# Differential attention: first row scaling, corner memset and scaling of the maximum left out, mask added on TensorE, squares on VectorE

## The reference

```python
q = partial_rope(rms_norm(q, q_norm_g), pos)
lam = exp(sum(lam_q1 * lam_k1)) - exp(sum(lam_q2 * lam_k2)) + lam_init
s = einsum('bqhd,bkhd->bhqk', q_blk, k) * DA_HEAD_DIM ** -0.5
allowed = k_chunk[None, :] <= q_chunk[:, None]        # chunks of 64 tokens
s = where(allowed, s, -inf)
p = softmax(s, axis=-1)                               # two maps per head pair
p = p[:, :, 0] - lam * p[:, :, 1]
o = einsum('bhqk,bkhe->bqhe', p, v)
o = rms_norm(o, subln_g, eps=1e-5) * (1.0 - lam_init)
return o.reshape(B, S, D) @ w_o
```

## Time and profile before

| what | value |
|---|---|
| median of 3 runs | 2335.53 us |
| lowest and highest | 2334.25 and 2338.73 us |
| the profiled execution, own time | 2339.69 us |
| its span in the trace | 2337.7 us |
| mean granted TensorE clock | 0.939 |
| PE, PEld busy | 2052.0, 1574.0 us |
| DVE, ACT, POOL busy | 795.4, 808.4, 857.0 us |

### The profile page before, as it was taken

One profiled execution on the slowest core, in us unless ns is written; L12 is line 12 of the kernel. 1 busy time (PEld: TensorE's weight loads), 2 busy tenths in 40 slices (PEclk: granted clock), 3 DMA queues, 4 the chain that ended last, 5 costly groups with the idle time before them and its releaser, 6 DMA issues.

```text
span 2337.7 us, 37067 instructions
## 1 busy us (share of the span) xinstructions
PE 2052.0 (88%) x15556; PEld 1574.0 (67%) x15556; DVE 795.4 (34%) x1209; ACT 808.4 (35%) x1051; POOL 857.0 (37%) x1112
## 2 busy tenths in 40 slices
PE   4897976668999999989997699999998999979897
PEld 3666866534777778865674377777887886748764
DVE  5487333334422221023447542222101133252333
ACT  6566232232334342132125434343212423242232
POOL 4263322210454545534330044545454523215430
PEclk8899999995999999999998789999999999889999
DMA  4101000020233333222110022333332211112110
GB/s 146 54 30 57 22 4 5 4 67 1 72 90 90 90 90 99 99 81 73 54 53 3 0 68 77 90 90 90 99 99 90 90 55 54 37 59 90 55 54 36
DMA packets 190707, 147.10 MB, mean 63 GB/s; under 512 B 6888, under 2 KB 188351, under 8 KB 190576
## 3 DMA queue, kind: packets, MB, share of 16 engines
q1 hardware_dynamic: 190576, 145.18, 20.3%
HBM read 143.06 MB, written 2.10 MB: 62 GB/s over the span
## 4 chain that ended last, share of the span: by engine, by line
PE 56%; issue 17%; POOL 14%; DVE 7%; ACT 5%; DMA 1%; SPq 0%; POOLq 0%; ACTq 0%; DVEq 0%
PE psum L2318 13%; POOL w_lo L1027 13%; PE psum L2320 12%; PE psum L2319 12%; PE psum L2481 4%; ACT w_hi L1159 1%; DVE X_lo L1692 1%; PE psum L2324 1%; PE psum L2743 1%; DVE col L2093 1%; PE psum L2706 1%; PE psum L2716 1%; PE psum L2394 1%; PE psum L2731 1%; PE psum L2900 1%
## 5 line engine op out<-in xcount | busy, mean ns | idle before, releaser
L1027 POOL TENSOR_TENSOR w_lo<-weight_raw,w_hi 128x256 fp32r<-128x256 f32 (+2 forms) x1048 | 772.0, 773 | 1227.7 <-ACT w_hi L1159 1227.5
L2318 PE MATMUL psum<-X_hi,w_hi 128*128 128x512 f32 x1528 | 633.2, 414 | 76.4 <-POOL w_lo L1027 42.1
L2320 PE MATMUL psum<-X_hi,w_lo 128*128 128x512 f32 x1528 | 608.4, 398 | 0.0
L2319 PE MATMUL psum<-X_lo,w_hi 128*128 128x512 f32 x1528 | 608.3, 398 | 0.0
L2318 PEld LDWEIGHTS psum<-X_hi,w_hi 128*128 128x128 f32 x1528 | 295.4, 193 | 184.0 <-issue 84.3
L1159 ACT ACTIVATE w_hi<-weight_raw 128x2048 fp32r<-128x2048 f32 (+2 forms) x134 | 249.6, 1863 | 376.5 <-PE psum L2320 364.0
L2319 PEld LDWEIGHTS psum<-X_lo,w_hi 128*128 128x128 f32 x1528 | 295.8, 194 | 64.8 <-issue 6.7
L2320 PEld LDWEIGHTS psum<-X_hi,w_lo 128*128 128x128 f32 x1528 | 294.6, 193 | 64.9
L1741 DVE TENSOR_TENSOR sgate<-rt,psum 128x512 f32<-128x512 f32 x44 | 30.2, 688 | 340.4 <-PE psum L2320 340.4
L2318 PE MATMUL psum<-hb_hi,w_hi 128*128 128x512 f32 x352 | 136.9, 389 | 0.0
L2319 PE MATMUL psum<-hb_lo,w_hi 128*128 128x512 f32 x352 | 136.9, 389 | 0.0
(11 more groups left out here) (447 smaller groups left out, 2624.3 us busy)
## 6 DMA issues: line engine op xcount, KB each, us to landing
weight_raw<-in_ffn_w_gu SPq DMA_DIRECT2D x88, 512.0 KB, 4.9
weight_raw<-in_l_w_in SPq DMA_DIRECT2D x45, 512.0 KB, 4.7
weight_raw<-in_ffn_w_down SPq DMA_DIRECT2D x40, 512.0 KB, 3.7
weight_raw<-in_kv_w SPq DMA_DIRECT2D x16, 512.0 KB, 4.0
weight_raw<-in_l_w_out SPq DMA_DIRECT2D x16, 512.0 KB, 4.0
weight_raw<-in_rw_w_k SPq DMA_DIRECT2D x8, 512.0 KB, 6.7
weight_raw<-in_rw_w_r SPq DMA_DIRECT2D x8, 512.0 KB, 4.0
weight_raw<-in_rw_w_v SPq DMA_DIRECT2D x8, 512.0 KB, 4.1
```

What stands on the lines that cost most here:

```text
L1027: ins = pool.tensor_tensor(l, r, h.bitcast(F32), ALU.subtract)
L2318: pe.matmul(ps, wh, xh, start=start, stop=False, skip_group_check=True)
L2319: pe.matmul(ps, wh, xl, start=False, stop=False, skip_group_check=True)
L2320: return pe.matmul(ps, wl, xh, start=False, stop=stop, skip_group_check=True)
```

## The change

The first row scaling goes: the first map stays as ACT's exponentials made it, and only the second is multiplied, by minus lambda times the first row sum over the second. The combined row is thereby larger by the first row sum. ACT writes that sum to a table `l1s`, and its square times 128e-5 enters the sum of squares as four small products on PE (`lsq`), in place of the constant epsilon. The memset of the corner goes: PE adds -1e30 there with a product of one row, the first row of the constant `blk` (64 ones, 64 zeros) by a row `neg` of 64 numbers, once for each map, behind both scores. The scaling of the maximum goes: the factor 1/8 moves into the gain of q's norm, and the reduction negates its own result. The squares of `oT` move from ACT to DVE, into the tiles of `aq`: seven of them into the loop, at the second query tile of a head pair from the third pair on, the last one behind it. PE adds up seven of the squares ahead of the last `values`, and the last one behind it.

```diff
--- before.py
+++ after.py
@@ -660,6 +660,9 @@
         PTs = a_("PTs", [P, 2, S])
         tq2 = a_("tq2", [P, 2, S])
         rth = a_("rth", [16, S])
+        l1s = a_("l1s", [P, TT, HEADS // 2])
+        lsq = a_("lsq", [P, TT, 16])
+        neg = a_("neg", [1, CH])
         n_hi = a_("n_hi", [16, S], F32R)
         n_lo = a_("n_lo", [16, S], F32R)
 
@@ -761,6 +764,7 @@
         rope_in, lam_in = sem("rope_in"), sem("lam_in")
         lam_row, lam_ready = sem("lam_row"), sem("lam_ready")
         sc_max = sem("sc_max")
+        lsq_ready = sem("lsq_ready")
         pc_ready = sem("pc_ready")
         hn_rot = sem("hn_rot")
 
@@ -1245,18 +1249,6 @@
                             last = act.activation(dst[:, 2 * i + m, 0:S], bank(b[m]), func)
                     last.then_inc(step_a, 1)
 
-            def head_scale(src, n, at, key, scale, eps, ready, count, hi):
-
-                for k in range(n):
-                    if k >= 2:
-                        act.wait_ge(hn_pe, hn_pe_count(at, k - 2))
-                    act.activation(xf[:, k % 2, :], src[:, k, 0:S], ACT.Square).then_inc(hn_a, 1)
-                wait_done(act, key)
-                act.activation(rt[0:16, :], psum[0:16, job_banks(key)[0], :], ACT.Sqrt, bias=cst[0:16, eps:eps + 1],
-                               scale=scale).then_inc(job_a, 1)
-                act.wait_ge(ready, count)
-                act.activation(hi[:, :], rt[0:16, :], ACT.Copy).then_inc(kn_h, 1)
-
             def layer_norm(n):
 
                 name = ("eo", "oo")[n]
@@ -1539,8 +1531,9 @@
                     for sub in range(2):
                         q = 2 * ((i + 2) % 3) + sub
                         ins = act.activation(Pb[:, q, 0:P * (tq + 1)], psum[:, b[sub], 0:P * (tq + 1)], ACT.Exp,
-                                             bias=col[:, 4 + q:5 + q], scale=HN ** -0.5,
-                                             accum_out=col[:, 16 + q:17 + q])
+                                             bias=col[:, 4 + q:5 + q],
+                                             accum_out=(l1s[:, tq, (i + 2) // TT:(i + 2) // TT + 1] if sub == 0 else
+                                                        col[:, 16 + q:17 + q]))
                     ins.then_inc(job_a, 1)
                 if i >= 0:
                     if i >= 1 and (i - 1) % TT == TT - 1:
@@ -1551,8 +1544,11 @@
                     act.activation(PTs[:, i % 2, 0:P * (tq + 1)], bank(job_banks(key)[0], P * (tq + 1)),
                                    ACT.Copy).then_inc(job_a, 1)
             empty(("ot", HEADS // 2 - 1), oT[:, HEADS // 2 - 1, :])
-            wait_job(act, ("ot", HEADS // 2 - 1))
-            head_scale(oT, KT, 16, ("osq",), 1.0 / P, C_EPS5, kn_f, 5, n_hi)
+            wait_done(act, ("osq",))
+            act.activation(rt[0:16, :], psum[0:16, job_banks(("osq",))[0], :], ACT.Sqrt, scale=1.0 / P
+                           ).then_inc(job_a, 1)
+            act.wait_ge(kn_f, 5)
+            act.activation(n_hi[:, :], rt[0:16, :], ACT.Copy).then_inc(kn_h, 1)
             for k in range(KT):
                 wait_job(act, ("oinv", k))
                 x_high1(XV["attn"], k, oT)
@@ -2020,6 +2016,8 @@
             wait_job(dve, ("lam",))
             link(dve.tensor_tensor(col[:, 2:3], col[:, 1:2], col[:, 0:1], ALU.subtract))
             dve.tensor_scalar(col[:, 3:4], col[:, 2:3], -LAM_INIT, None, ALU.add)
+            dve.memset(neg[0:1, :], -1e30)
+            dve.tensor_scalar(col[:, 13:14], pcol("da_q_norm_g"), HN ** -0.5, None, ALU.mult)
             link(dve.tensor_scalar(col[:, 12:13], pcol("da_subln_g"), 1.0 - LAM_INIT, None, ALU.mult))
 
             def scaled(name, dst, steps):
@@ -2049,7 +2047,7 @@
                                           ALU.subtract).then_inc(kn_l, 1)
                     elif what == "hinv":
                         wait_done(dve, key)
-                        dve.scalar_tensor_tensor(out=src[:, k, :], in0=src[:, k, :], scalar=pcol(g),
+                        dve.scalar_tensor_tensor(out=src[:, k, :], in0=src[:, k, :], scalar=g,
                                                  in1=bank(job_banks(key)[0]), op0=ALU.mult,
                                                  op1=ALU.mult).then_inc(job_d, 1)
                     elif what == "rot":
@@ -2065,21 +2063,28 @@
                 dve.wait_ge(hn_rot, 8 * n_ + k + 1)
 
             for n in range(32):
-                att_part(0, "q", aq, "da_q_norm_g", n)
+                att_part(0, "q", aq, col[:, 13:14], n)
                 if n % 8 == 7:
                     scaled("kk", ak, (n // 8,))
             wait_product(dve, "kk")
             for n in range(32):
-                att_part(1, "k", ak, "k_norm_g", n)
+                att_part(1, "k", ak, pcol("k_norm_g"), n)
             n_i = HEADS // 2 * TT
+
+            def head_square(k):
+
+                wait_job(dve, ("ot", k))
+                dve.tensor_tensor(aq[:, k, :], oT[:, k, :], oT[:, k, :], ALU.mult).then_inc(hn_a, 1)
+
             for i in range(-2, n_i):
                 if i >= 0:
                     N = P * (i % TT + 1)
                     q = 2 * (i % 3)
                     wait_job(dve, ("sc", i))
-                    link(dve.reciprocal(col[:, 16 + q:18 + q], col[:, 16 + q:18 + q]))
-                    dve.tensor_scalar(Pb[:, q, 0:N], Pb[:, q, 0:N], col[:, 16 + q:17 + q], None, ALU.mult)
-                    link(dve.tensor_tensor(col[:, 17 + q:18 + q], col[:, 17 + q:18 + q], col[:, 3:4], ALU.mult))
+                    link(dve.reciprocal(col[:, 17 + q:18 + q], col[:, 17 + q:18 + q]))
+                    link(dve.scalar_tensor_tensor(out=col[:, 17 + q:18 + q], in0=col[:, 17 + q:18 + q],
+                                                  scalar=col[:, 3:4], in1=l1s[:, i % TT, i // TT:i // TT + 1],
+                                                  op0=ALU.mult, op1=ALU.mult))
                     dve.scalar_tensor_tensor(out=Pb[:, q, 0:N], in0=Pb[:, q + 1, 0:N],
                                              scalar=col[:, 17 + q:18 + q], in1=Pb[:, q, 0:N], op0=ALU.mult,
                                              op1=ALU.add).then_inc(pc_ready, 1)
@@ -2089,11 +2094,16 @@
                     N = P * ((i + 2) % TT + 1)
                     q = 4 + 2 * ((i + 2) % 3)
                     wait_done(dve, ("sc", i + 2))
-                    link(dve.memset(psum[0:64, b:b + 2, N - CH:N], -1e30))
-                    link(dve.tensor_reduce(col[:, 14:16], psum[:, b:b + 2, 0:N], AX.X, ALU.max))
-                    dve.tensor_scalar(col[:, q:q + 2], col[:, 14:16], -(HN ** -0.5), None,
-                                      ALU.mult).then_inc(sc_max, 1)
-                    dve.wait_ge(sc_max, i + 3)
+                    dve.tensor_reduce(col[:, q:q + 2], psum[:, b:b + 2, 0:N], AX.X, ALU.max,
+                                      negate=True).then_inc(sc_max, 1)
+                if i > TT and i % TT == 1:
+                    head_square(i // TT - 1)
+            sums = l1s[:, :, :].rearrange("p t k -> p (t k)")[:, :, None]
+            dve.scalar_tensor_tensor(out=lsq[:, :, :].rearrange("p t (k a) -> p (t k) a", a=2),
+                                     in0=sums.to_broadcast([P, TT * HEADS // 2, 2]), scalar=1e-5 * P,
+                                     in1=sums.to_broadcast([P, TT * HEADS // 2, 2]), op0=ALU.mult,
+                                     op1=ALU.mult).then_inc(lsq_ready, 1)
+            head_square(HEADS // 2 - 1)
             head_inverse(("osq",), 5, n_hi, n_lo)
             for k in range(KT):
                 key = ("oinv", k)
@@ -2393,14 +2403,6 @@
                     pe.wait_ge(sq_ready, 8 * i + k + 1)
                     ins = pe.matmul(bank(6), c_("ones"), square_buffer(i)[:, k % 2, :], start=k == 0, stop=k == KT - 1)
                     ins.then_inc(sq_used if k < KT - 1 else job_done, 1)
-
-            def head_sum(key, n, at, sel):
-
-                b = begin(key)
-                for k in range(n):
-                    pe.wait_ge(hn_a, at + k + 1)
-                    pe.matmul(psum[0:16, b, :], c_(sel, 16, 16 * k), xf[:, k % 2, :], start=k == 0,
-                              stop=k == n - 1).then_inc(hn_pe if k < n - 1 else job_done, 1)
 
             pe.wait_ge(cst_in, 16)
             for k in range(KT):
@@ -2728,8 +2730,11 @@
                 b = begin(("sc", i))
                 for sub in range(2):
                     rows = slice(64 * sub, 64 * sub + 64)
-                    ins = pe.matmul(psum[:, b + sub, 0:P * (tq + 1)], aq[rows, hd, P * tq:P * tq + P],
-                                    ak[rows, hd, 0:P * (tq + 1)], start=True, stop=True)
+                    pe.matmul(psum[:, b + sub, 0:P * (tq + 1)], aq[rows, hd, P * tq:P * tq + P],
+                              ak[rows, hd, 0:P * (tq + 1)], start=True, stop=False, skip_group_check=True)
+                for sub in range(2):
+                    ins = pe.matmul(psum[:, b + sub, P * tq + CH:P * tq + P], c_("blk")[0:1, :], neg[0:1, :],
```

(19 more changed lines are left out.)

## The result

The changed kernel takes **2367.28 us** (median of 4 runs, 2363.69 to 2372.11) where the kernel before takes 2334.89 (4 runs on the same chip): a ratio of **1.0137 [1.0111, 1.0164]**. That is 32.4 us slower; 6.9 us faster was forecast, and the time lies outside the range. The profiled execution took 2363.69 us, 3.6 under its median.

What follows compares the result with a forecast made beforehand. No engine is full in the attention loop; its chain is mostly PE (41%) and DVE (about 37%), with part of the time at half clock. Loop -2.1 and tail -4.8 make -6.9 us: 2335.5 to 2328.6 us, own range 2322 to 2335.

Steps and rivals of the forecast that it cites:

- the clock's share left as it is: Attention loop: forecast -2.1 us with the half-clock share of the time unchanged, about 34%, mean granted clock near 0.83.
- Rival B: Loop: masks make PE the bound at half clock, so the kernel gets slower, 2344.2 us; chance 0.30.
- B's price: Half-clock share 0.34 to 0.70: loop +11.4 us, tail -2.7, together +8.7; each tenth of share 3.8 us.
- third: Part of the loop's half-clock time taken as other engines' pace; only PE's two thirds was priced as changing with the clock.
- Rival A: Loop: PE's idle gaps shrink and the clock stays up; -17.9 us with the tail, 2317.6 us; chance 0.15.
- Rival C: Loop: masks nearly free at 0.10 us a step; -11.5 us with the tail, 2324.0 us; chance 0.08.
- The mask's own price: Between scores and maximum: one-row masks take 0.36 us a step at full clock, 0.72 at half; +7.0 us on the chain.
- a mask costs more than 0.5 us at full clock: One of the signs, written beforehand, by which the forecast would be wrong; it concerns the mask in the loop.
- Memset, row scaling, max scaling: DVE work removed from the loop's chain: memset and max scaling together -7.6 us, row scaling -2.9 us.
- complete path: Second path through two loop steps, 5.72 us at full clock; gains 0.04 per two steps, -0.6 us over the loop.
- Squares at cost 0: Seven squares on DVE in the loop, 4.8 us, hidden in DVE's 25.1 us of waits for scores; up to +4.8 if exposed.
- Tail: Behind the loop up to the root, 13.7 us before: forecast -4.8 us, between -6.9 at full and -2.7 at half clock.

Runs made afterwards that it cites:

- e9: Changed kernel with the mask product over 16 rows instead of one, the added rows zero, still two passes; 2373.64 us, ratio 1.0152.
- e3: Changed kernel with the mask product over 128 rows instead of one, the added rows zero, still two passes; 2330.59 us, ratio 0.9999.
- e5: Changed kernel without any mask, the causal masking inside the diagonal block left out; 2306.58 us, ratio 0.9897.
- e12: Kernel before without row and max scaling, squares on ACT behind the loop, memset kept; 2334.51 us, ratio 0.9994; repeated 2330.57 us, 0.9978.
- e1: Changed kernel with the memset back in place of the mask products; 2326.19 us, ratio 0.9968; repeated 2325.2 us, 0.9952.
- e2: Kernel before with only the memset replaced by the one-row mask products on PE; 2363.79 us, ratio 1.0145.
- e7: Kernel before with only the squares moved to DVE and seven sums ahead of the last values; 2335.95 us, ratio 1.0027.
- e6: Changed kernel with the mask in a single pass (fp32r) over 128 rows into 64 output partitions; 2320.09 us, ratio 0.9953.
- e11: Changed kernel with the single-pass 128-row mask into 64 partitions and seven sums at the head of the last two steps; 2315.70 us, ratio 0.9908.

## Why the prediction was wrong, step by step

**The step that failed is the mask on TensorE, and with it "the clock's share left as it is".** Rival B named the mechanism, its evidence (16-row products at 0.50 for 20 us) and its mark (grant under 0.75 and PE busy over nine tenths; 0.60 and 91% came), and had 0.30. The trace before spoke both ways. In this stretch ahead of the loop 11 of PE's 67 products are of 16 rows, 4.9 us of its 20.0, and the clock is 1.00:

```profile
1120.00:1140.00 20.00, 20.00 (x67) 11.59 (x67) 18.97 (x28) 1.82 (x1) 3.14 (x4) 1.00 0.16 53
```

So few-row products don't always bring the lower level, and B was a rival and no certainty. But the forecast gave no reason for a change of nothing. What it held against B, that PE's pauses get shorter, came true (PE busy 91% of the loop, 72% before) and did not keep the clock up; e9 shows that in this loop 16 rows act as one does. B's price was also far too small, +8.7 where +34.3 came in loop and tail. Two terms of it fell short. The share went from 0.34 to 0.80, not 0.70. And a tenth of share costs 6.6 to 7.6 us in a full PE queue (32.1 us between 0.38 at e3 and 0.80, or 27.6 without the 4.5 above), not 3.8: e3 already has PE busy 90.0 of 102.5 us, so other engines' pace holds much less than the "third" that was left out.

**Rival A**, the clock stays up, is refuted: PE was busy 91% of the changed kernel's loop at 0.60 and 76% of e5's at 0.91. The Trainium skill, "TensorE: Matmul & The Clock Gate", Part 1, says that activity releases the throttle; no run here bears that out for busy time as such. **Rival C** fell with the mask's price.

**The mask's own price**, 0.36 and 0.72, was 0.58 and 1.04. The upper bound of 0.12 for a load came from loads with products of a single column; a load of one row with its 64-column product takes 0.145 and 0.26 (a quarter of the mask step). By "a mask costs more than 0.5 us at full clock" the text called this too.

**Memset, row scaling, max scaling.** The chain's terms of -3.8 for max scaling and -2.9 for the row scaling make -6.7; e12 measures -6.6 in the loop. The number was right, and halving it towards the "complete path" was not. How far the agreement is luck stays open, as the clock rose from 0.83 to 0.86, which the terms don't hold. The memset was put at -3.8; e1 against e5 gives -9.2, as the clock also rises from 0.81 to 0.91 without it.

**Squares at cost 0.** Whether that held in the changed kernel, no run shows: DVE has waits enough there, yet e2, with the scalings and without squares in the loop, is 3.2 us shorter. In the kernel before the squares cost 9.9 us (e7), beside the smaller work of DVE at most 2.8 (e12 to e1: 90.3 to 93.1, with the seven sums' order in it). Of the 25.1 us of waits one of 12.2 lay nearly whole ahead of the loop, and in e7 there was none around the square shown: a sum of waits is no cover.

**Tail**: -3.4 (-3.6 from e12 to e1) for -4.8, inside its ends but for the wrong reason. The stretch was at a clock of 0.94, so the high end, -6.9, should have come. The term that failed is 14 x 0.23 us for the seven sums: 0.23 is a single-pass product's, and these are fp32. In the changed kernel's tail, in order of time:

```profile
1360.05 6.88 PE L2772 MATMUL psum<-aq,cst 128*16 128x512 f32 x14
...
1366.87 1.16 PE L2748 MATMUL psum<-PTs,av 128*128 128x128 f32 x8
...
1369.44 1.03 PE L2772 MATMUL psum<-aq,cst 128*16 128x512 f32 x2 [0.44 <-DVE aq L2077]
```

Fourteen of them hold PE 6.8 us at mostly the higher level, 0.49 each; with that in place of 3.2 the forecast's full-clock sum of 6.8 becomes 10.4, which is what the tail took. Setup and DMA: nothing showed.

## What to carry to other kernels

Before work is moved to TensorE, ask what it does to the granted clock and not only how long it takes: products of one or sixteen rows, between large ones in an already full queue, held the clock at 0.60 to 0.63 and cost 50.7 and 46.9 us where the same mask in one pass over 128 rows, into 64 partitions, cost 5.7. Padding the contraction with zero rows cost no time and gave 32.1 us back. And read cover at the place where the new work will stand: a total of waits over a loop, or a duration from a product with another number of passes, prices nothing.

## What the runs showed of the hardware that was not expected

- In this loop the granted clock depends on how many rows the mask products fill, at the same instructions and columns and with loads of 0.52 us in all three: 0.60 with one row, 0.63 with 16, 0.81 with 128 (134.6, 130.8 and 102.5 us of loop).
- It is not PE's busy share that goes with the clock: 91% busy at 0.60, 88% at 0.81 (e3), 81% at 0.88 (e6), 84% at 0.91 (e11).
- Small work on another engine moved the clock too: seven squares on DVE, 4.8 us, took it from 0.83 to 0.77 and with it PE's busy time in the loop from 70.1 to 77.8 us for the same products and one sum of 1.0 us (e7).
